# One chunk of the conditioning product moves from GpSimd to VectorE, in a kernel of two transformer blocks

## The reference, cut to what matters

```
c_act = silu(c)                          # (1, 1024)
mod   = c_act @ w_ada[0] + b_ada[0]      # w_ada: 1024 x 6144
sh1, sc1, g1, sh2, sc2, g2 = split(mod, 6)
```

## Time and profile before

| | us |
|---|---|
| median of 3 runs | 1091.37 (1088.86 to 1094.81) |
| profiled execution, its own time | 1096.7 |
| its span, first to last instruction | 1094.8 |
| TensorE busy | 916.7 (84%) |
| VectorE busy | 540.0 (49%) |
| GpSimd busy | 76.4 (7%) |
| stretch of the first block's mixers, weave included | about 92 to 199 |

### The profile page before, as it was taken

The page is one execution under the profiler, slowest core; times in us unless marked ns, Lnnn a source line. Parts: engine busy times, 40 slices in busy tenths (PEclk is TensorE's granted clock), DMA queues, the critical chain, the costliest instruction groups (busy, mean ns, idle before and its releaser), DMA issues.

```text
span 1094.8 us, 19087 instructions
## 1 busy us (share of the span) xinstructions
PE 916.7 (84%) x8318; PEld 706.3 (65%) x8318; DVE 540.0 (49%) x1004; ACT 346.5 (32%) x678; POOL 76.4 (7%) x113
## 2 busy tenths in 40 slices
PE   5999999999999998999999988666667575667665
PEld 4686888489999887988989965333334333334332
DVE  2456588847888856798866643111212111211121
ACT  2431255236767534545553341000101000000001
POOL 3102710000000000231001000000000000000000
PEclk9999999989999999999999999888878888888888
DMA  9343472674653565786436989999999999999994
GB/s 331 133 141 133 151 269 80 231 230 154 200 185 120 222 223 211 235 246 217 133 128 231 429 325 427 429 429 429 428 430 426 430 429 429 427 429 429 429 429 184
DMA packets 76089, 316.69 MB, mean 289 GB/s; under 512 B 3983, under 2 KB 27824, under 8 KB 63456
## 3 DMA queue, kind: packets, MB, share of 16 engines
q1 hardware_dynamic: 71236, 302.24, 70.1%
q0 software_dynamic: 4624, 13.14, 4.0%
q10 hardware_dynamic: 140, 0.04, 0.0%
HBM read 312.24 MB, written 1.06 MB: 286 GB/s over the span
## 4 chain that ended last, share of the span: by engine, by line
PE 58%; DMA 27%; DVE 8%; ACT 3%; issue 2%; SPq 0%; POOL 0%; DVEq 0%; ACTq 0%
PE ps L461 56%; DMA w<-in_w_up 18%; DMA w<-in_w_gate 6%; DMA w<-in_w_down 2%; DVE sp L1812 2%; DMA w<-in_w_in 1%; DMA rot<-q 1%; PE ps L550 0%; PE ps L2625 0%; DVE acc L875 0%; ACT sp L1803 0%; ACT hts L2720 0%; ACT sd L2125 0%; PE ps L982 0%; PE ps L2057 0%
## 5 line engine op out<-in xcount | busy, mean ns | idle before, releaser
L461 PE MATMUL ps<-w,xg 128*32 128x256 f32 x2048 | 158.8, 474 | 108.0 <-DMA w<-in_w_up 84.9
L461 PE MATMUL ps<-hb,sp 128*128 128x256 f32 x1824 | 226.7, 285 | 0.0
L461 PEld LDWEIGHTS ps<-hb,sp 128*128 128x128 f32 x1824 | 220.8, 190 | 3.9 <-issue 2.8
L461 PEld LDWEIGHTS ps<-w,xg 128*32 128x32 f32 x2048 | 85.1, 131 | 180.1 <-issue 156.2
L1812 DVE TENSOR_TENSOR sp<-w,sp 128x1024 fp32r<-128x1024 f32 x122 | 144.3, 1220 | 39.6 <-ACT sp L1803 39.6
L1803 ACT ACTIVATE sp<-w 128x1024 fp32r<-128x1024 f32 x122 | 122.1, 1051 | 44.1 <-PE ps L461 44.1
L2784 DVE TENSOR_TENSOR cst<-ps,cst 64x256 f32<-64x256 f32 x32 | 13.7, 427 | 227.5 <-ACT cst L2716 227.5
L2716 ACT ACTIVATE cst<-ps 64x256 f32<-64x256 f32 x32 | 12.1, 378 | 328.1 <-PE ps L461 328.1
L2799 DVE TENSOR_TENSOR ost<-ps,cst 32x256 f32<-32x256 f32 x120 | 50.4, 420 | 100.1 <-PE ps L461 97.3
L461 PE MATMUL ps<-w,hts 128*32 128x256 f32 x1024 | 62.1, 382 | 13.9 <-ACT hts L2720 11.4
L461 PE MATMUL ps<-ht,w 128*128 128x256 f32 x256 | 62.9, 400 | 2.2 <-DMA w<-in_w_in 2.2
(11 more groups left out here) (398 smaller groups left out, 1150.9 us busy)
## 6 DMA issues: line engine op xcount, KB each, us to landing
w<-in_w_down SPq DMA_DIRECT2D x36, 2048.0 KB, 35.7
w<-in_w_gate SPq DMA_DIRECT2D x32, 2048.0 KB, 28.2
w<-in_w_up SPq DMA_DIRECT2D x32, 2048.0 KB, 32.5
w<-in_w_in SPq DMA_DIRECT2D x14, 2048.0 KB, 9.2
w<-in_w_up SPq DMA_DIRECT2D x22, 1024.0 KB, 7.7
w<-in_w_ada SPq DMA_DIRECT2D x8, 2048.0 KB, 9.1
w<-in_w_out SPq DMA_DIRECT2D x4, 2048.0 KB, 8.2
w<-in_w_ada POOLq DMA_DIRECT2D x8, 768.0 KB, 5.3
```

Source lines behind the costliest of these rows:

```text
L461: return q.eng.matmul(o, l, r, start=start, stop=stop, skip_group_check=True)
```

## The change

The first chunk goes from GpSimd to VectorE. `ada_first_ve` is a generator of eight instructions like `ada_ve`, it writes straight to `acc[0]`, and `ada_k` now ends at 8. It is placed between the rest of chunk 2 and chunk 3, and in every fourth step `g` (3, 7, 11, ...) a second instruction of `rest` is taken, which makes 45 places in the 36 steps for what are now 36 instructions. `rwkv_gp` no longer calls `ada_gp`. The loads, their slots and their order in SP's queue are as they were.

```
         def ada_done(i):
-            return (s["ada_d"], 8 * i) if i else (s["ada_k"], 15)
+            return (s["ada_d"], 8 * i) if i else (s["ada_k"], 8)
...
-        def ada_gp(q):
+        def ada_first_ve(q):
             e, w = q.eng, v(chunks["ada", 0].ap, 8)
             q.wait_ge(*chunks["ada", 0].tok)
             q.wait_ge(s["cp"], 2)
-            for k in range(8):
-                e.tensor_tensor(w[:, k, :], w[:, k, :], bc(cpv[:, k, 0:1], [128, 512]), MUL).then_inc(s["ada_k"], 1)
-            for k in range(0, 8, 2):
-                q.wait_ge(s["ada_k"], k + 2)
-                e.tensor_tensor(w[:, k, :], w[:, k, :], w[:, k + 1, :], ADD).then_inc(s["ada_k"], 1)
-            for k in (0, 4):
-                q.wait_ge(s["ada_k"], 10 + k // 2)
-                e.tensor_tensor(w[:, k, :], w[:, k, :], w[:, k + 2, :], ADD).then_inc(s["ada_k"], 1)
-            q.wait_ge(s["ada_k"], 14)
             q.wait_ge(s["hs_mm"], 2)
             q.wait_ge(s["rq_mm"], 3)
-            e.tensor_tensor(acc[0], w[:, 0, :], w[:, 4, :], ADD).then_inc(s["ada_k"], 1)
+            e.tensor_scalar(acc[0], w[:, 0, :], cpv[:, 0, 0:1], None, MUL).then_inc(s["ada_k"], 1)
+            yield
+            for k in range(1, 8):
+                q.wait_ge(s["ada_k"], k)
+                e.scalar_tensor_tensor(out=acc[0], in0=w[:, k, :], scalar=cpv[:, k, 0:1], in1=acc[0], op0=MUL, op1=ADD).then_inc(s["ada_k"], 1)
+                yield
...
             e.memset(MBd, 0.0).then_inc(s["r_z"], 1)
-            ada_gp(q)
             q.wait_ge(s["r_mm"], RN["off", 1])
...
-            rest = in_turn([second] + [ada_ve(q, i) for i in range(3, NVEC)])
+            rest = in_turn([second, ada_first_ve(q)] + [ada_ve(q, i) for i in range(3, NVEC)])
             for g in range(A1_STEPS):
                 attn_ve(q, g)
                 next(rest, END)
+                if g % 4 == 3:
+                    next(rest, END)
                 yield
```

## The result

The changed kernel takes 1110.24 us (median of 4 runs, 1109.34 to 1111.75) against 1093.02 (median of 4, 1088.86 to 1094.81) for the one before: ratio 1.015, 95% interval 1.0127 to 1.0173. It is slower, by 16.4 us at that ratio. Forecast were 10.5 us, 1101.9, and the range 1098 to 1107.5 does not hold the result. The direction was right and so was the wait for the load, the size was 6 us short.

A forecast was written before the change was run, and what follows sets the result against it. It took TensorE arithmetic, then expert weights over DMA, as the bounds. Shift +9.2 us at the copy for which TensorE waits, plus 1.3 for late second calls, gave +10.5 on 1091.4: 1101.9 us, range 1098 to 1107.5.

The forecast's parts named there:

- The shift at the copy of 171.24: VectorE's copy into t, for which TensorE waits: claimed 9.2 us later, from the load wait and added second calls.
- Chunk 6's load not waited for: After chunk 5's end: VectorE may wait 0.5 us for this load, covered by 3.5 us before TensorE needs the norm: 0.
- GpSimd's earlier end worth 0: GpSimd's removed 19.4 us on chunk 0 were beside the path; an earlier free GpSimd starts nothing earlier: 0.
- The instructions of 1418 ns: Three VectorE scalar_tensor_tensor beside GpSimd's arithmetic return to 750 ns, 2.0 us around 125 to 130: worth 0, at most 2.0.
- I add 0, and keep 0 to 3: Lower TensorE clock at the restart after 7.2 us idle: 1.7 us of work, nearly all covered, so 0, range 0 to 3.
- my margin of 1.5 us: At TensorE's restart, VectorE reaches the copy of 160.25 about 1.5 us after TensorE's product is ready, covering the slower clock.
- VectorE's second calls in steps 27 and 28: Second call of step 27 and call of step 28, inside the VectorE piece from 188.3 to 193.2: +1.3 us.
- second calls of steps 19 and 23: 0: VectorE is off the path from 171.8 to 188 with 2.61 us idle before 187.73, so these calls add 0.
- The loads share the engines: Rival: with three loads in flight, chunk 3 lands after 14.2 us rather than 9.3: +15.4 us, 1106.8; chance 0.15.
- The restart at half clock: Rival: TensorE's small products slowed until the end of the inverse, 3 us on top: +13.5 us, 1104.9; chance 0.08.
- VectorE did not catch up: Rival was that VectorE catches up after the wait, shorter ScalarE and TensorE waits returning up to 4 us: +6.5; chance 0.08.
- Not slower: Rival: VectorE freed from GpSimd gains 2.0 us, 1089.4, if chunk 3's load lands under 2.4 us from issue; chance 0.05.

The follow-up runs named there:

- no_product: The kernel before without GpSimd's 14 products and additions on chunk 0, leaving out its sum over k: ratio 0.9992.
- dummies: The changed kernel with 14 more TensorE products into unused columns, ahead of waits in the recurrence's late steps: ratio 1.0115 against the kernel before.
- before_dummies: The kernel before with 14 more TensorE products into unused columns, ahead of waits in the recurrence's late steps: ratio 1.0020.
- calls_to_15: The changed kernel with the second call kept in steps 3, 7, 11, 15 and removed from 19, 23, 27: ratio 1.0087 against the kernel before.
- four_products: The changed kernel with 4 more TensorE products, all ahead of TensorE's read of st: ratio 1.0101 against the kernel before.
- swapped: The changed kernel with chunk 0 summed ahead of chunk 2 on VectorE, second calls kept: ratio 1.0044 against the kernel before.
- one_call: The changed kernel without the second call in every fourth step, 36 instructions in 36 steps: ratio 1.0110 against the kernel before.
- early: Against the kernel before, VectorE sums chunk 0 in its own buffer where it waits for TensorE, no second calls in the loop: ratio 0.9988.

## Why the prediction was wrong in size, point by point

**Right, with their numbers.** The load order: SP issued three loads at the end of chunk 0 (forecast 154.0, measured 151.83 + 1.39 = 153.2). Landing of the first with two behind it: 9.5, forecast 9.3. VectorE's stall 9.06, forecast 8.9. TensorE idle 7.35, forecast 7.2. The shift at the copy of 171.24: 8.8, forecast 9.2. Chunk 6's load not waited for, forecast up to 0.5 us and off the path. GpSimd's earlier end worth 0, shown by no_product. The instructions of 1418 ns went back to 750, with no gain: the 51.90 us piece has the same length. The later stage bound by DMA moved as a whole: the first long load of `w_gate` in the chain of waits begins at 699.50 instead of 684.95, a shift of 15.9.

**The step that failed: the clock, "I add 0, and keep 0 to 3".** I looked for the lower clock only at the restart. There it came (0.65, 0.50, 0.57 to 168) and it cost next to nothing, since the shift at the copy is even under the forecast. But my margin of 1.5 us was not there: the copy at 167.73 is the one of 160.25, and VectorE waited 0.46 us for TensorE's product, which was the later of the two. It came a second time, in the late steps of the recurrence. From TensorE's read of `st` to the first `w_out` product the kernel before took 199.01 - 181.90 = 17.1 us, the changed one 214.13 - 190.39 = 23.7: +6.6, where the sum had +1.3 for VectorE's second calls in steps 27 and 28. The three parts are 8.8 at the copy of 171.24, 1.1 from there to the read of `st`, and these 6.6, together the 16.5 of the distance. The sum had 9.2, 0 and 1.3.

What the clock is worth, the two kernels with the added products tell. From the read of `st` to the first `w_out` product they take 210.89 - 192.49 = 18.4 us (dummies) and 200.54 - 182.15 = 18.4 us (before_dummies), with the late steps at 2.4 GHz in both. So the second calls of steps 27 and 28 cost nothing there, and all of the 6.6 us goes with the clock. Over the whole distance it is (210.89 - 85.71) - (200.54 - 84.50) = 125.18 - 116.04 = 9.1 us against 16.5 without the products, a difference of 7.4. By the ratios of the timed runs it is 1.0115 - 1.0020, 10.4 us against 16.4, a difference of 6.0. So 6 to 7.4 us is an estimate of the clock's part, since it takes the products to cost the same in both. The two stretches of twelve products above, 1.55 to 2.82 and 1.50 to 2.77, are 2.5 us of it.

**The step under it: "second calls of steps 19 and 23: 0".** I called VectorE off the path from 171.8 to 188, because the chain showed other engines there, and counted on its 2.61 us of idle time before 187.73. But the copy into `st` (181.01 before) stands ahead of that idle time, and TensorE, busy until then, reads `st` 0.05 us after it ends (181.01 + 0.84 against 181.90). There was no slack at that place. The two calls made it late, and TensorE stood idle for 1.07 us. As a term of the sum that is 1.1 instead of 0. Its larger effect is that the low clock began there. Taking out the calls of 19, 23 and 27 (calls_to_15) brought the clock back for the whole stage, and filling the idle time with four products (four_products) for the next 11 us.

**What is shown and what is not.** Shown: the wait alone gives 8.5 us and leaves the late steps at the upper clock. The added calls without the wait give the low stretch (swapped). With the calls out, or with TensorE kept busy, it goes. Not shown: what exactly brings the clock down. Before `st` the idle time was 1.07 and 1.08 in changed and swapped, and the clock fell in both. But idle times of 1.08 and 1.13 in one_call and of 1.34 and 1.13 in calls_to_15, 12 to 15 us further on in the same steps, left it up. At the step of line 982, an idle time of 0.68 was followed by the low clock before, and the same 0.68 was not in early. So the length of one idle time does not decide it, and that the idle time before `st` is the trigger rests on what happens when it is taken away, in a profile or two of each kernel.

**The rivals.** "The loads share the engines" had the right size, 15.4, by a mechanism that did not occur: chunk 3 landed after 9.5 us, and it was the third load that took 19.2. "The restart at half clock" was the right kind of cost, at the wrong place and with 3 us too small. VectorE did not catch up (8.8 of 9.2). "Not slower" fell with the load, which took 9.5 us where its condition was under 2.4. The agreement on speed that I gave it is a rough one: a product by GpSimd took 1.00 us (8.02 / 8) and its last addition 1.31, VectorE's `scalar_tensor_tensor` 0.75.

The rule of the Trainium skill, TensorE: Matmul & The Clock Gate, "Why this matters for your kernels", against idle gaps between bursts of matmuls, held at the restart: TensorE stood still for 7.35 us and the clock was at 0.50 when it went on. The idle time before `st`, 1.07 us, is shorter than the gaps that it warns of, and there the clock fell all the same.

## What to carry to other kernels

A buffer that is freed later delays every load behind it in the queue, and the first user of that load pays: look at when a moved sum ends, not only at what it costs. When a step is called off the path because its engine has idle time, check that the idle time comes before the first instruction that another engine is waiting for, with the gap in the trace at that instruction. And where TensorE runs few and small products, a new wait can have a second price, that of the sparse work behind it at half clock: here 10 us of it in swapped, 20 in the changed kernel, and none in the waits that left the clock up. Keep it in the range, and look in the profile after whether the clock fell.

## What was not expected of the hardware

The lower clock lasted 20 us (0.50 from 192 to 208) with TensorE busy for all of the 16 us between, in 72 products:

```profile
192.00:208.00 16.00, 16.00 (x72) 13.78 (x69) 7.85 (x18) 5.87 (x15) 0.00 (x0) 0.50 0.11 27
```

Before, the same kind of steps stayed at 1.0 with 61 products in 8 us (184 to 192). In the changed kernel the lower clock was left at 211.8, half a us ahead of the first products of 512 columns, in swapped at 194.4 in the middle of the same steps. After the 7 us of complete standstill the clock was back within some 5 us of dense small products. So in the changed kernel an idle time of 1.07 us was followed by a loss of some 6.6 us, and one of 7.35 us by next to none beyond itself.
